# Sample group of the latent attention: which operand stands in the TensorE array when the values are summed

## The reference

```python
k_mla, v_mla = mla_keys(lat, kr, p)          # 8 heads: keys of 96, values of 64
s = jnp.einsum('bqhd,bkhd->bhqk', q, k).astype(jnp.float32) * (MLA_QK ** -0.5)
...
w = jax.nn.softmax(s, axis=-1).astype(v.dtype)
return jnp.einsum('bhqk,bkhd->bqhd', w, v)   # the step of the change, for 32 queries
```

## Time and profile before

| | us |
|---|---|
| median of 3 runs | 1413.21 (1411.27 to 1417.32) |
| the profiled execution | 1413.97 |
| its span, first to last instruction | 1411.9 |
| PE busy | 1361.3 (96% of the span) |
| DVE busy | 778.1 (55%) |
| ACT busy | 635.5 (45%) |
| mean granted TensorE clock | 0.993 of full speed |

### The profile page before, as it was taken

The page is one execution under the profiler, slowest core; times in us unless marked ns, Lnnn a source line. Parts: engine busy times, 40 slices in busy tenths (PEclk is TensorE's granted clock), DMA queues, the critical chain, the costliest instruction groups (busy, mean ns, idle before and its releaser), DMA issues.

```text
span 1411.9 us, 20830 instructions
## 1 busy us (share of the span) xinstructions
PE 1361.3 (96%) x8354; PEld 1110.0 (79%) x8354; DVE 778.1 (55%) x1153; ACT 635.5 (45%) x932; POOL 102.0 (7%) x92
## 2 busy tenths in 40 slices
PE   6999999999999999999899999999999999999998
PEld 5995666899999767677589856569999987676774
DVE  4425756433435247887673267454343343678875
ACT  5317855422224245665452377553232232456651
POOL 0301000000000011100333000000000000101002
PEclk9999999999999999999999999999999999999999
DMA  8224030023215449998821200302133163699965
GB/s 245 84 80 155 1 120 0 31 90 119 82 60 200 169 164 382 409 416 341 280 87 61 83 2 1 120 1 77 57 106 119 51 233 138 234 402 410 415 237 205
DMA packets 97384, 228.27 MB, mean 162 GB/s; under 512 B 16459, under 2 KB 66661, under 8 KB 84326
## 3 DMA queue, kind: packets, MB, share of 16 engines
q1 hardware_dynamic: 85222, 179.42, 35.1%
q0 software_dynamic: 7904, 32.64, 6.4%
q10 hardware_dynamic: 4176, 15.08, 2.7%
HBM read 198.56 MB, written 33.79 MB: 165 GB/s over the span
## 4 chain that ended last, share of the span: by engine, by line
PE 89%; DVE 4%; ACT 4%; issue 2%; DMA 2%; DVEq 0%; POOL 0%; ACTq 0%; POOLq 0%
PE ps L885 10%; PE ps L887 10%; PE ps L886 10%; PE ps L1404 7%; PE ps L1380 4%; PE ps L1381 4%; PE ps L1382 4%; PE ps L914 3%; PE ps L917 3%; PE ps L1209 2%; PE ps L911 2%; PE ps L1265 2%; PE ps L1267 2%; PE ps L1266 2%; PE ps L1365 2%; PE ps L1065 2%
## 5 line engine op out<-in xcount | busy, mean ns | idle before, releaser
L2022 DVE TENSOR_TENSOR work<-work,ps 128x544 f32<-128x544 f32 x48 | 34.6, 721 | 208.7 <-ACT work L1815 208.7
L1815 ACT ACTIVATE work<-ps 128x544 f32<-128x544 f32 x48 | 30.0, 625 | 244.7 <-PE ps L887 244.7
L783 POOL DMA_INDIRECT rows_back<-xrow_d,row_of x32 | 34.5, 1079 | 1067.7 <-DVE row_of L2458 842.0
L886 PE MATMUL ps<-xn_r,ksv_r 128*128 128x272 f32 x384 | 110.8, 288 | 0.0
L886 PE MATMUL ps<-xn_r,work_r 128*128 128x272 f32 x384 | 110.7, 288 | 0.0
L1382 PE MATMUL ps<-ew_r,rows_tok_r 128*128 128x512 f32 x256 | 99.9, 390 | 0.0
L2022 DVE TENSOR_TENSOR ew_r<-ew,gu_hi_a_r 128x2048 fp32r<-128x2048 f32 x32 | 73.0, 2286 | 17.0 <-ACT gu_hi_a_r L1838 17.0
L886 PEld LDWEIGHTS ps<-xn_r,ksv_r 128*128 128x128 f32 x384 | 72.2, 188 | 0.0
L886 PEld LDWEIGHTS ps<-xn_r,work_r 128*128 128x128 f32 x384 | 72.2, 188 | 0.0
L1838 ACT ACTIVATE gu_hi_a_r<-ew 128x2048 fp32r<-128x2048 f32 x32 | 60.6, 1908 | 5.6 <-ACT yo_b L1885 5.6
L1404 PE MATMUL ps<-ew,acts 128*128 128x512 f32 x128 | 57.9, 595 | 2.5 <-DVE acts L2589 2.5
(11 more groups left out here) (420 smaller groups left out, 3868.5 us busy)
## 6 DMA issues: line engine op xcount, KB each, us to landing
wr<-in_w_in SPq DMA_DIRECT2D x68, 512.0 KB, 4.6
ew<-in_w_exp_gate SPq DMA_DIRECT2D x32, 1024.0 KB, 6.8
ew<-in_w_exp_up SPq DMA_DIRECT2D x32, 1024.0 KB, 10.4
ew<-in_w_exp_down SPq DMA_DIRECT2D x32, 1024.0 KB
wr<-in_w_out SPq DMA_DIRECT2D x16, 512.0 KB, 4.1
rows_d<-yo_a ACTq DMA_DIRECT2D x14, 512.0 KB
rows_d<-yo_b ACTq DMA_DIRECT2D x14, 512.0 KB
rows_d<-in_zeros POOLq DMA_DIRECT2D x10, 512.0 KB, 9.5
```

Source lines behind the costliest of these rows:

```text
L886: mm(out_[h], w_hi, x_lo[:, c], start=False, stop=False, skip_group_check=True)
L2022: return v_.tensor_tensor(o_, a, b, op)
```

## The change

The sample's values are summed the other way about. Four heads' transposed softmax weights (128 columns, four heads of 32 queries) stand in the array and the values of four heads (256 columns) move. That multiplies each head's weights with all four heads' values; only the blocks on the diagonal, 32 rows by 64 columns, are wanted. DVE copies these blocks out (`sample_blocks`, four copies of 32 rows by two times 64 columns, to `sample_rows`), PE transposes the result once (`sample_turn`), and the copy to `ybr` that was there reads it as before. So that the transposed rows come out in the right order, unit x now holds the heads x, x + 2, x + 4, x + 6 where it held 4x to 4x + 3. The semaphores `pv_mm` and `o_nrm` get one more count per layer, and waits on later groups are shifted by one (`signals`).

```diff
+        sample_rows = work[:, 5632:5632 + P]
...
                         for i in range(4):
-                            ins = mm(ps[DEC * i:DEC * i + DEC, n % 4, 0:288], qT[0:QK, 4 * x + i, SEQ:T], kT[0:QK, 4 * x + i, SEQ:KEYS],
+                            ins = mm(ps[DEC * i:DEC * i + DEC, n % 4, 0:288], qT[0:QK, 2 * i + x, SEQ:T], kT[0:QK, 2 * i + x, SEQ:KEYS],
...
                     if h is None:
-                        for a in range(HEADS):
-                            pb, g, c = 64 * (a % 2), a // 4, VD * a
-                            dst = ps[pb:pb + 64, 6 + k % 2, DEC * (a // 2):DEC * (a // 2) + DEC]
-                            for j in (1, 2):
-                                q = P * j + DEC * (a % 4)
-                                mm(dst, vv_tail[j][:, c:c + VD], pt_s[:, g, q:q + DEC], start=(j == 1), stop=False, skip_group_check=True)
-                            q = DEC * (a % 4)
-                            ins = mm(dst, vv_tail[0][0:DEC, c:c + VD], pt_s[0:DEC, g, q:q + DEC], start=False, stop=True, skip_group_check=True)
+                        for g in range(2):
+                            for j in (1, 2, 0):
+                                m = P if j else DEC
+                                vals = vv_tail[j][0:m, :].rearrange("p (a g n) -> p a g n", a=4, g=2)[:, :, g, :]
+                                ins = mm(bank(6 + k % 2, 4 * VD, P, 4 * VD * g), pt_s[0:m, g, P * j:P * j + P], vals,
+                                         start=(j == 1), stop=(j == 0), skip_group_check=True)
...
+                def sample_turn(k):
+                    pe.wait_ge(o_nrm[0], at(o_nrm, l, k + 1))
+                    nc.tensor.transpose(bank(6 + k % 2, P), sample_rows, ident).then_inc(pv_mm[0], 1)
...
                     turn(n)
+                    if n - 2 == MLA_FIRST[1 + MLA_GROUPS.index(None)]:
+                        sample_turn(MLA_GROUPS.index(None))
...
+                def sample_blocks(k):
+                    dve.wait_ge(pv_mm[0], at(pv_mm, l, k + 1))
+                    for a in range(4):
+                        q, c = DEC * a, VD * a
+                        ins = v_.tensor_copy(sample_rows[q:q + DEC, :].rearrange("p (g n) -> p g n", g=2),
+                                             ps[q:q + DEC, 6 + k % 2, :].rearrange("p (g n) -> p g n", g=2)[:, :, c:c + VD])
+                    ins.then_inc(o_nrm[0], 1)
...
                     if n + 3 < NU:
                         neg_max(n + 3)
+                    if n - 1 == MLA_FIRST[1 + MLA_GROUPS.index(None)]:
+                        sample_blocks(MLA_GROUPS.index(None))
```

More of the change, by code:

```diff
@@ L392, in hybrid_streaming_encoder @@
         pr_nrm = sem("pr_nrm", 2)
-        pv_mm = sem("pv_mm", HEADS + 1)
+        pv_mm = sem("pv_mm", HEADS + 2)
         den = sem("den", 2 * HEADS)
-        o_nrm = sem("o_nrm", HEADS + 1)
+        o_nrm = sem("o_nrm", HEADS + 2)
         pw_high = sem("pw_high", 6)
@@ L490, in unit, with signals @@
             return k, MLA_GROUPS[k], x
+        def signals(groups):
+            return groups + (groups > MLA_GROUPS.index(None))
         def by_act(n):
@@ L1194, in values @@
                     if k >= 2:
-                        pe.wait_ge(o_nrm[0], at(o_nrm, l, k - 1))
+                        pe.wait_ge(o_nrm[0], at(o_nrm, l, signals(k - 1)))
                     if h is None:
-                        for a in range(HEADS):
-                            pb, g, c = 64 * (a % 2), a // 4, VD * a
-                            dst = ps[pb:pb + 64, 6 + k % 2, DEC * (a // 2):DEC * (a // 2) + DEC]
-                            for j in (1, 2):
-                                q = P * j + DEC * (a % 4)
-                                mm(dst, vv_tail[j][:, c:c + VD], pt_s[:, g, q:q + DEC], start=(j == 1), stop=False, skip_group_check=True)
-                            q = DEC * (a % 4)
-                            ins = mm(dst, vv_tail[0][0:DEC, c:c + VD], pt_s[0:DEC, g, q:q + DEC], start=False, stop=True, skip_group_check=True)
+                        for g in range(2):
[4 more added lines that the diff above has]
+                                         start=(j == 1), stop=(j == 0), skip_group_check=True)
                     else:
@@ L1742, in weights_out @@
                     if k >= 2:
-                        act.wait_ge(pv_mm[0], at(pv_mm, l, k - 1))
+                        act.wait_ge(pv_mm[0], at(pv_mm, l, signals(k - 1)))
                     f(pt[:, k % 2, 0:t + 1, P * t:P * t + P], ps[:, 4 + n % 2, :].rearrange("p (j n) -> p j n", j=4)[:, 0:t + 1, :], ACT.Copy).then_inc(pt_act[0], 1)
@@ L1750, in denominators @@
                     if half == 0:
-                        act.wait_ge(pv_mm[0], at(pv_mm, l, k + 1))
+                        act.wait_ge(pv_mm[0], at(pv_mm, l, signals(k + 1) if k > MLA_GROUPS.index(None) else k + 1))
                         f(dst, ps[d:d + 64, 6 + k % 2, :], ACT.Ln).then_inc(den[0], 1)
@@ L1783, in _ @@
                 high(11)
-                act.wait_ge(o_nrm[0], at(o_nrm, l, HEADS + 1))
+                act.wait_ge(o_nrm[0], at(o_nrm, l, HEADS + 2))
                 for j in range(12, 16):
@@ L2280, in normalise @@
                     if h is None:
-                        dve.wait_ge(pv_mm[0], at(pv_mm, l, k + 1))
+                        dve.wait_ge(pv_mm[0], at(pv_mm, l, k + 2))
                         v_.tensor_copy(ybr[:, 2:6, SEQ:T], ps[:, 6 + k % 2, 0:4 * DEC].rearrange("p (k n) -> p k n", k=4)).then_inc(o_nrm[0], 1)
@@ L2301, in _ @@
                         if k >= 2:
-                            dve.wait_ge(pv_mm[0], at(pv_mm, l, k - 1))
+                            dve.wait_ge(pv_mm[0], at(pv_mm, l, signals(k - 1)))
                         v_.tensor_copy(pt[:, k % 2, 0:x + 1, P * x:P * x + P], ps[:, 4 + n % 2, :].rearrange("p (j n) -> p j n", j=4)[:, 0:x + 1, :]).then_inc(pt_ev[0], 1)
```

## The result

| | us |
|---|---|
| kernel before, median of 8 runs | 1411.44 (1410.57 to 1417.32) |
| changed kernel, median of 8 runs | 1419.78 (1417.27 to 1426.72) |
| ratio | 1.006, 95% interval 1.0043 to 1.0076 |
| changed kernel, profiled execution | 1426.72 (span 1424.9, mean granted clock 0.989) |

The forecast was 1404.3 us, faster. The changed kernel is 0.6% slower. The profiled execution is the slowest of its eight, so the 13 us between the two profiled executions are more than the change costs (8 us between the medians).

What follows compares the result with a forecast made beforehand. PE, 89% of the chain of waits, was taken as the bound. Gains of 4.5 us in layer 0 and 4.35 in layer 1, 8.9 off 1413.97, gave 1405.1, or 1404.3 us against the median; range 1401.8 to 1409.5.

Steps and rivals of the forecast that it cites:

- Step (1): Sample's values, layer 0: the 24 narrow matmuls go, 5.28 us of PE, all on the path.
- Step (2): Sample's values: six wide matmuls, 12 records, come in at 2.58 us, with no surcharge for runs of 64 columns.
- rival C: In `values(4)`, runs of 64 columns starve the moving operand: 1419.8 us at four times the cost; chance 0.04.
- Step (3): PE behind `values(4)`: short work until 228.27, then a wait for DVE's copies before `sample_turn`, put at 0.37 us.
- Step (7): Put at nothing: head order, shifted counts, `normalise(4)`, DMA queues; nothing behind the stage takes back the gain.
- Step (4): DVE's four copies out of PSUM take 0.84 us at 0.19 pitch; 1.08 end to end.
- Steps (5) and (6): After the copies: `sample_turn` 0.11 us, other work 2.60; next values at 231.6, between PE's 231.35 and DVE's 231.91.
- step (6): Next head's values wait for DVE's eviction of `turn(21)`, 231.91 at the latest; taken 231.6, 4.5 and 4.35 us less.
- A: Around the sample's values the clock falls all the same: gain only 3.4 us, 1409.8 us; chance 0.12.
- B: DVE begins the next head later, giving back 1 to 2 us in each layer: 1407.3 us; chance 0.10.

Runs made afterwards that it cites:

- e1_count: Changed kernel with the o_nrm wait of `sample_turn` one count lower and `values(5)` keeping the wait on `normalise(3)`; 1410.73 us, 0.9985 of the kernel before.
- e5_act: e2_late with two of the four block copies moved from DVE to ACT; 1410.62 us, 0.9976 of the kernel before.
- c3_late: e2_late unchanged, traced a second time; 1411.97 us.
- x_heads: Kernel before with only the new order of heads in the two sample units, narrow matmuls kept; 1413.84 us, 0.9996 of the kernel before.
- e4_order: e3_behind with the four wide matmuls of 128 rows first, then the two of 32, which alters the sums; 1410.42 us, 0.9977 of the kernel before.
- e2_late: e1_count with `sample_turn` one unit later, behind `turn(21)`; 1409.79 us, 0.9971 of the kernel before.
- x_split: Kernel before with its 24 narrow matmuls handed out in four parts, ahead of `turn(19)` to `turn(22)`; 1415.85 us, 1.0017 of the kernel before.
- c1_after: Changed kernel, unchanged, timed and traced again; 1419.3 us, 1.0053 of the kernel before.
- x_pause: Kernel before, narrow matmuls kept, with only PE's wait for `normalise(3)` behind `turn(20)` added; 1418.28 us, 1.0044 of the kernel before.
- e3_behind: Changed kernel with the four copies moved to n = 22, `sample_turn` behind `values(5)`, `normalise(4)` at n = 24; 1408.83 us, 0.9972 of the kernel before.

## Why the prediction was wrong, by its steps

**Step (1), the narrow matmuls go:** right, and so was the reading that they cost the clock. In no trace of e1 to e5, or in c3_late, is the clock low anywhere in the stage's middle in either layer; in the three traces of before and that of x_heads it is, in both.

**Step (2), 2.58 us for the wide ones:** 3.19. The rate of the moving columns was nearly right (in e4_order eight records of one height take 1.82 us, 0.23 each for the 0.215 of the forecast, so rival C is out). What was missing is the change between 128 and 32 rows, where the weight loads pause for 0.33 us. By e4_order each costs 0.2 us; three lie inside the run and the fourth at its end, and three times 0.2 is the difference of 0.6.

**Step (3), the wait in front of `sample_turn`: this is the step that failed.** It took for granted that the wait ends with the copies. By the count it ends with `normalise(3)`, one signal later on DVE. The prediction gave 0.37 us of waiting; the trace shows 2.18, and e1_count 0.47 once the count is right. Step (7) repeats the error in the words that the shifted counts "stand for the same events". They didn't for the new wait itself, nor for that of `values(5)`: it asks for the fourth count, which was `normalise(3)` and is now the copies, and only the high count of `sample_turn` ahead of it kept `values(5)` behind `normalise(3)`. The error could have been read off the code before the run: DVE's program has the copies at n = 19 and `normalise(3)` at n = 20, and the front of this document names both places.

**Step (4), four copies in 0.84 us:** 1.19, with 0.27 to 0.29 us for each and a pitch of 0.30. The pitch of 0.19 that I took from the earlier trace rows is that between a copy and an instruction of another kind; four copies in a row went end to end. The upper bound, 1.08, was below it too. The Trainium skill, "VectorE: DVE Perf Modes", the section on the TRN2 errata, would have given an estimate of 1.03, which is nearer. Whether it was the like shape, the small operand or the rows (each copy starts 32 rows below the one ahead of it) that kept them from overlapping, no run tells.

**Steps (5) and (6), the order behind it and DVE as the next bound:** right in kind. e1_count's stretch is 7.39 against 6.57: 0.6 too little in step (2), the rest DVE, whose evictions end PE's wait for the next values (0.53 us), as step (6) had it.

**Step (7), the gain passes whole:** not quite, even with the count mended: e1_count's 1410.7 us are 6 above the forecast and outside its range. The stretch of before averages 10.6 us (three traces and x_heads's, eight stretches), e1_count's is 7.39 and e2_late's 7.25: 6.4 to 6.7 us for the two layers. By their ratios the two kernels are 2 and 4 us faster. In those eight the clock is low for 6.8 us six times and for 3.4 twice, half of which is lost: 6.0 us an execution on average, where the trace behind the prediction had 6.8. The clock loss fell by 3.4 us (e1) and 4.3 (e2) and not by 6.0. If the stage keeps the clock in every execution, as in those that were traced, these kernels lose more of it in other places (one is 1219 to 1221 us, in three of the six traces of e1 to e5 and c3_late, in none of those of before and its variants). The rest, by contrast, is 0.3 to 0.5 us higher than before, although the stage is a little shorter at equal clock too: with the low part at half, before's stretch is 10.95 - 3.4 = 7.6 us, or 9.60 - 1.7 = 7.9 from its third trace, and x_split's layer 0, at full clock, 8.37 with what its other order adds, against 7.25 to 7.39.

One place where this is lost again can be named. In layer 1, ahead of the experts, PE waits for a DMA that gathers rows; a row of the kernel before and one of c1_after:

```profile
1223.70 1.16 PE L1365 MATMUL ps<-con,rows_back 128*128 128x128 f32 x8 [0.56 <-DMA rows_back<-xrow_d,row_of]
...
1227.50 1.16 PE L1374 MATMUL ps<-con,rows_back 128*128 128x128 f32 x8 [1.76 <-DMA rows_back<-xrow_d,row_of]
```

The wait is 0.56 to 1.50 us in the six traces with narrow matmuls (1.0 on average) and 1.76 to 1.98 in the eight with wide ones (1.8). This is a wait behind the stage, which the step had excluded from the DMA share of one window. What makes the gather late there, and why other places lose more of the clock, is open. Most of the gain is that the clock isn't lost in the stage.

**The sizes.** In the changed kernel itself the rest went up by 4.2 us and the clock loss by 2.6. By estimate the stretches account for 1.9 to 2.5 of the 4.2 (10.76 less half of 3.4, and 11.72 less half of the 6.1 of low clock in it, against 7.6 to 7.9 twice). The longer wait for the gather is another 0.8. And at the end of layer 0's experts PE waits longer for DVE, in before and in c1_after:

```profile
701.76 0.47 PE L856 MATMUL ps<-yo_b_r,ew_r 128*128 128x512 f32 x1 [1.27 <-DVE gu_hi_b_r L2565]
...
705.11 0.47 PE L861 MATMUL ps<-yo_b_r,ew_r 128*128 128x512 f32 x1 [2.36 <-DVE gu_hi_b_r L2584]
```

It is 2.56 and 2.36 us in the two traces of the changed kernel, and 0.90 to 1.59 in the five of before, x_heads and x_pause, so about 1.2 more. Together these are 3.9 to 4.5 us, which covers the 4.2. What links the two later waits to the change, no run tells.

**Rivals.** A, that the clock falls all the same, came true in part: it fell, but later (232.0 for 228.4 us), in a stretch that the forecast didn't contain, behind a pause that the count made. The run with the short pause, e1_count, kept it, so by itself the rival's reason (0.4 us of stall among short transposes) wasn't enough. Its price was worked out with too short a low stretch in layer 1: a window mean of 0.85 is 0.3 us at half clock, so the clock was low from 924.7 to 931.5 us, 6.8 and not 6.4. B was seen in e3_behind and e4_order (1.16 us) and, by 0.1 us, in e2_late. C didn't happen. The kernel came out slower by a way that none of the three names.

**What is best.** e2_late beats both kernels, 0.9971 of before (4 us; 3 by the medians); e3_behind and e5_act are level with it and more intricate.

## What to carry to other kernels

When a semaphore counts events from several places of an engine's program, work out for each new wait which event gives its last count, in the order in which that engine issues them; here one count was the difference between a kernel some 2 us faster and one 7 to 8 us slower. A short pause of PE can cost more than its length when it takes the clock with it (two pauses of 1.38 us, one in each layer, and about 5 us of time in x_pause), so a wait added behind a long run of PE work is priced with the clock. And take a stretch of low clock from several executions before its repair is forecast.

## What the runs showed of the hardware

- The granted clock fell from 1.00 to 0.50 with PE busy 1.00 of 1.00 us, in both layers of all three traces of the kernel before: while a run of narrow fp32 matmuls (64 columns standing, 32 moving) was under way in two of them (228.4 and 924.7 us in the first), and 1.0 and 0.7 us after its end in the third (229.9 and 926.2). With six wide ones for the same sums and no long pause behind them it stayed at 1.00, in six traces (e1 to e5, c3_late).
- The same program lost the clock at a place in one execution and not in another (the kernel before at 870 us in its first trace, not in its third); over 91 executions of it one line, 1404.6 + 1411 x (1 - mean granted clock), gives its times to within 1.1 us (standard deviation; 2.3 without it).
- fp32 matmuls that alternate between 128 and 32 rows of weights show 0.33 us without a weight load at each change: 3.19 us with four changes (one at the end), 2.79 with two, for the same 12 records, so 0.2 us a change.
- Four copies of 32 x 128 from PSUM took 1.19 us on DVE in a row (0.30 from start to start). Two on DVE and two on ACT, side by side, took 0.58 and 0.55.
